# Spreading a hosted modulation chunk over both weight chunks of a feed-forward step, and over the last two chunks of a projection group

## The reference

```python
ada = jax.nn.silu(c) @ w_ada[l] + b_ada[l]              # first block, 6 x 1024 numbers per layer
sh1, sc1, g1, sh2, sc2, g2 = jnp.split(ada, 6, axis=-1)
...
h = x * (1.0 + sc2) + sh2
g, u = jnp.split(h @ w_in, 2, axis=-1)                  # feed-forward
y = (jax.nn.silu(g) * u) @ w_out
...
m = jax.nn.silu(cond) @ w_ada + b_ada                   # second block, 9 x 1024 numbers,
                                                        # for c and for c_ctx: two vectors
```

## Time and profile before

| | us |
|---|---|
| median of 3 runs | 2665.36 |
| lowest and highest | 2662.78, 2667.13 |
| profiled execution | 2660.99 |
| its span | 2659.1 |
| granted TensorE clock, mean | 0.988 of full speed |
| PE busy | 2518.5 (95%) |
| DVE busy | 1741.2 (65%) |
| ACT busy | 1085.0 (41%) |
| DMA packets, 16 engines | 413.85 MB, 156 GB/s over the span |

### The profile page before, as it was taken

How to read it: one execution, slowest core, us unless ns; L and a number is a source line. 1 busy time by engine, 2 the same in 40 slices (tenths; PEclk the granted TensorE clock), 3 DMA queues, 4 the chain that set the end, 5 groups by cost and what they waited for, 6 DMA issues and landing times.

```text
span 2659.1 us, 41471 instructions
## 1 busy us (share of the span) xinstructions
PE 2518.5 (95%) x16280; PEld 2145.2 (81%) x16280; DVE 1741.2 (65%) x3313; ACT 1085.0 (41%) x2119; POOL 136.7 (5%) x92
## 2 busy tenths in 40 slices
PE   4879999899999999999998999999999999999999
PEld 3858998888997888887766788888788887777998
DVE  7678777677777677546778756554665543678754
ACT  2445545445444333223356333332333323446554
POOL 1000100000100111000000011100011100000010
PEclk9989999999999999999999999999999999999999
DMA  8926876926662444444510444434344433613653
GB/s 285 282 100 211 273 246 196 281 75 203 211 223 89 153 168 162 140 137 131 152 33 10 143 150 143 143 122 132 111 143 143 139 110 132 156 64 117 217 180 122
DMA packets 354893, 413.85 MB, mean 156 GB/s; under 512 B 24754, under 2 KB 291931, under 8 KB 354635
## 3 DMA queue, kind: packets, MB, share of 16 engines
q1 hardware_dynamic: 352496, 404.13, 47.3%
q0 software_dynamic: 1120, 5.70, 0.6%
q10 hardware_dynamic: 1082, 1.38, 0.2%
HBM read 409.56 MB, written 5.27 MB: 156 GB/s over the span
## 4 chain that ended last, share of the span: by engine, by line
PE 80%; DVE 11%; DMA 4%; ACT 3%; issue 2%; SPq 0%; ACTq 0%; DVEq 0%
PE bank L901 79%; DVE ada_partial L1632 3%; DVE weight_lo L695 2%; PE bank L1208 2%; DMA raw_weights<-in_w_in_ab_dram 1%; DMA raw_weights<-in_w_in_cd_dram 1%; ACT weight_hi L1295 1%; DMA raw_weights<-in_w_ffn_in_dram 1%; DVE bank L1952 1%; DVE X L1856 0%; ACT H_hi L1396 0%; DVE rstd L1899 0%; DVE probs L1971 0%; ACT X L1403 0%; DVE bias L1903 0%
## 5 line engine op out<-in xcount | busy, mean ns | idle before, releaser
L695 DVE TENSOR_TENSOR weight_lo<-raw_weights,weight_hi 128x512 fp32r<-128x512 f32 x1024 | 771.2, 761 | 797.0 <-ACT weight_hi L1295 782.0
L1295 ACT ACTIVATE weight_hi<-raw_weights 128x512 fp32r<-128x512 f32 x1024 | 632.6, 629 | 1231.9 <-PE bank L901 1125.7
L901 PE MATMUL bank<-H_hi,weight_hi 128*128 128x256 f32 (+1 forms) x2832 | 954.9, 337 | 36.2 <-DVE weight_lo L695 19.2
L901 PE MATMUL bank<-H_lo,weight_hi 128*128 128x256 f32 (+1 forms) x2832 | 938.7, 331 | 0.0
L901 PE MATMUL bank<-H_hi,weight_lo 128*128 128x256 f32 (+1 forms) x2832 | 938.1, 331 | 0.0
L901 PEld LDWEIGHTS bank<-H_hi,weight_hi 128*128 128x128 f32 x2832 | 540.0, 191 | 122.1 <-issue 58.6
L901 PEld LDWEIGHTS bank<-H_hi,weight_lo 128*128 128x128 f32 x2832 | 540.2, 191 | 50.7
L901 PEld LDWEIGHTS bank<-H_lo,weight_hi 128*128 128x128 f32 x2832 | 540.6, 191 | 47.1 <-issue 0.5
L1632 DVE SCALAR_TENSOR_TENSOR ada_partial<-raw_weights,silu_c,ada_partial 128x512 f32<-128x512 f32 x616 | 442.0, 745 | 1.4 <-DVE ada_partial L1632 0.2
L901 PE MATMUL bank<-hidden_hi,weight_hi 128*128 128x256 f32 (+1 forms) x1056 | 356.5, 338 | 4.0 <-DVE weight_lo L695 4.0
L901 PE MATMUL bank<-hidden_hi,weight_lo 128*128 128x256 f32 (+1 forms) x1056 | 354.1, 335 | 0.0
(11 more groups left out here) (191 smaller groups left out, 1848.7 us busy)
## 6 DMA issues: line engine op xcount, KB each, us to landing
raw_weights<-in_w_ada_dram SPq DMA_DIRECT2D x120, 1024.0 KB, 5.6
raw_weights<-in_w_ffn_up_dram SPq DMA_DIRECT2D x88, 1024.0 KB, 5.6
raw_weights<-in_w_ffn_in_dram SPq DMA_DIRECT2D x44, 1024.0 KB, 6.1
raw_weights<-in_w_ffn_down_dram SPq DMA_DIRECT2D x32, 1024.0 KB, 5.0
raw_weights<-in_w_in_dram SPq DMA_DIRECT2D x18, 1024.0 KB, 5.9
raw_weights<-in_w_ffn_out_dram SPq DMA_DIRECT2D x16, 1024.0 KB, 7.7
raw_weights<-in_w_in_ab_dram SPq DMA_DIRECT2D x12, 1024.0 KB, 9.3
raw_weights<-in_w_in_cd_dram SPq DMA_DIRECT2D x12, 1024.0 KB, 8.3
```

Source lines behind the costliest of these rows:

```text
L695: eng.tensor_tensor(WL[:, p.g % SPLIT, 0:p.kt * CW].rearrange("p (t n) -> p t n", n=CW), raw_ap(ch.n, ch.kt, CW)[:, p.k0:p.k0 + p.kt, :], ...
L901: return pe.matmul(o, w, x, start=start, stop=stop, skip_group_check=True)
L1295: act.activation(WH[:, p.g % SPLIT, 0:p.kt * CW].rearrange("p (t n) -> p t n", n=CW), raw_ap(ch.n, ch.kt, CW)[:, p.k0:p.k0 + p.kt, :], ACT ...
```

## The change

In a hosted step of `ffn_in` without `more`, DVE reads the a chunk in eight shares over the g loop and the u loop, not in four over the g loop. With four row tiles and eight shares, every second share does one tile: those at the second and fourth piece of each loop. The slot is released after the last share, at the end of the u loop. The order of the chunks (g, a, u) is not changed. In `proj` the a chunk moves ahead of c1 in the chunk order (c0, a, c1, c2), on SP too, and DVE reads it in seven shares beside the splits of c1's and c2's loops; the last share stands behind the group's last split, as before. Steps with `more`, the stages with one chunk per group, and qkv are as before.

```diff
--- before.py
+++ after.py
@@ -535,9 +535,10 @@
             ready=act_ready.take(11), host=host)
         groups = []
         for m in range(4):
-            cs = [chunk("g", view(w_out), k, min(KC, NF - k), CW * m) for k in range(0, NF, KC)]
-            groups.append(Rows(chunks=cs, host=ada_chunk() if steps[-1].host and m < 3 else None,
-                               grp=group("dve")))
+            cs = [chunk("g", view(w_out), 0, KC, CW * m)]
+            a1 = ada_chunk() if steps[-1].host and m < 3 else None
+            cs += [chunk("g", view(w_out), k, min(KC, NF - k), CW * m) for k in range(KC, NF, KC)]
+            groups.append(Rows(chunks=cs, host=a1, grp=group("dve")))
         add("proj", hosted=len(ADA) if bare else None, n=n, groups=groups, ada=ada, gate=gate, half=half, hidden=True,
             first=first,
             ready=act_ready.total, x_out=x_ready.take(1), tile6=x_tile.take(1),
@@ -815,8 +816,8 @@
                 for g in s.groups:
                     for ch in g.chunks:
                         load_one(ch)
-                    if g.host:
-                        load_one(g.host)
+                        if g.host and ch is g.chunks[0]:
+                            load_one(g.host)
 
         sp.wait_ge(out_cp, 4)
         sp.dma_start(out.rearrange("a (q p) d -> p (a q) d", p=P), OUTR[:, :, :]).then_inc(out_dma, 16)
@@ -1636,13 +1637,13 @@
                 chain.wait(closed["acc"][nv - 1])
                 dve.sem_inc(ada_used, 1)
 
-        def ahead_of(at, f, host=None, hook=None):
+        def ahead_of(at, f, host=None, hook=None, first=0, parts=None):
 
             n = len(f(at.u).pieces)
             for i in range(n):
                 ahead(at, lambda k: f(k).pieces[i], split, late)
                 if host:
-                    ada(at, host, i, n)
+                    ada(at, host, first + i, parts or n)
                 if hook:
                     hook(i)
 
@@ -1809,8 +1810,15 @@
             n = s.n
 
             def step(at):
-                ahead_of(at, lambda k: s.steps[k].g, (lambda k: s.steps[k].host) if s.steps[at.u].host else None)
-                ahead_of(at, lambda k: s.steps[k].u, (lambda k: s.steps[k].more) if s.steps[at.u].more else None)
+                st = s.steps[at.u]
+                host = (lambda k: s.steps[k].host) if st.host else None
+                if st.more:
+                    ahead_of(at, lambda k: s.steps[k].g, host)
+                    ahead_of(at, lambda k: s.steps[k].u, lambda k: s.steps[k].more)
+                else:
+                    half = KC // PIECE
+                    ahead_of(at, lambda k: s.steps[k].g, host, None, 0, 2 * half)
+                    ahead_of(at, lambda k: s.steps[k].u, host, None, half, 2 * half)
                 used(at, lambda k: s.steps[k].u.pieces[-1])
                 dve.wait_ge(silu_g.sem, at(lambda k: s.silu + k + 1))
 
@@ -1831,8 +1839,13 @@
             dve.wait_ge(ada_out, s.need)
             for m, g in enumerate(s.groups):
                 last = g is s.groups[-1]
+                at, parts = 0, sum(len(ch.pieces) for ch in g.chunks[1:])
                 for ch in g.chunks:
-                    if last and ch is g.chunks[-1]:
+                    if s.hidden and not last:
+                        ahead_of(one, lambda _: ch, (lambda _: g.host) if g.host and ch is not g.chunks[0] else None, None,
+                                 at, parts)
+                        at += len(ch.pieces) if ch is not g.chunks[0] else 0
+                    elif last and ch is g.chunks[-1]:
                         n_ahead = len(ch.pieces) - 1
                         for i, p in enumerate(ch.pieces[:-1]):
                             ahead(one, lambda _: p, split, late)
```

## The result

The changed kernel takes 2785.7 us (median of 4, 2784.1 to 2791.1) against 2664.6 (median of 4); the ratio is 1.0457, interval 1.0445 to 1.0469. The forecast was 2753, slower, with a stated range of 2715 to 2790. The profiled execution took 2784.06, its span is 2782.2, 123.1 us more than before.

What follows compares the result with a forecast made beforehand. PE was taken as the bound, busy 95% of the span. Terms 39.9 + 18.1 + 20.9 + 8.8 - 9.9 + 10 = 88 us on 2661.0 gave 2749, median 2753; range 2715 to 2790, its own 2735 to 2775.

Steps and rivals of the forecast that it cites:

- rival B: 256-column gaps: the clock falls at every stall, 37 us instead of 10, 2780 us; chance 0.14.
- Release, landing, split: Hosted `ffn_in`, after PE finishes u (S): u' issued at S + 2.2 us, landing 5.3, splitting 1.4; PE starts at S + 8.9.
- (1): `ffn_in` at 256 columns: PE idles 2.85 us on average before u' at 14 places, 39.9 us.
- (2): `ffn_in` at 512 columns: u' ready at S + 9.6 us against 10.88, so 29 places cost 0.
- (3): `proj`: c1' queues behind a', PE waits; 18.1 us first layer, 20.9 second layer, 8.8 at 512 columns.
- (4): Second layer's steps and `proj`: spreading DVE's work may remove losses of 5.4 and 4.5 us, a 9.9 us gain.
- (5): 256 columns: PE's clock falls behind some of 22 gaps, 0.46 us each on average, 10 us.
- Rival A: Whole change: the slot is not what binds and spreading helps, 2655 us, faster; chance 0.03.
- Rival C: Hosted steps and `proj`: DMAs issued together share engines, so all land at about 8.4 us, 2851 us; chance 0.08.
- Rival E: Whole change: no difference, DMAs already late before and PE had unseen slack; chance 0.03.
- Rival D: `proj`: the queue is shorter than assumed, or c1' lands with a'; its cost is a third, 2721 us; chance 0.12.

## Why the prediction was right, and where not

The mechanism was right: SP waits for a's slot, the weights behind it land late, and PE waits at the forecast places. Its added waiting was 86 us; the forecast without the clock term, the gain taken off, was 78. The sum was 33 us short, mainly by the clock term, and only the allowance for rival B in the stated range covers the measured time.

- **Release, landing, split** (S + 2.2, 5.3, 1.4): right. The chain has 310.45 - 309.01 = 1.4 us from the start of DVE's split to the issue (0.67 earlier ACT's), 5.20 for the landing, and with the gaps filled every first-layer step is 14.7 to 15.3 against 14.66. The fit that the prediction quotes from the Trainium skill (DMA: Bandwidth & Descriptors, Anatomy of one DMA) is stated there for DMAs that GpSimd issues; SP issues these, and their 5.2 us decide.
- **(1)** 14 places at 256 columns: right in place and number. The places of the second layer and the last feed-forward show it best: steps 1 and 2 there are 16.8 to 18.3 us, and the later ones together are within 0.6 us of those before (+0.5 and -0.6). In size, PE idled 3.1 us in the mean of the first layer's ten, for 2.85 forecast. In the last feed-forward one gap was 4.1 us, because u' landed 6.5 us after its issue.
- **(2)** 512 columns covered: right. Steps are 21.76 and 22.60 as in the earlier trace rows in all three feed-forwards, but for two of the third (21.94 and 22.35), and no stage's ten steps take longer than before.
- **(3)** `proj`: right. 17.6 us in the first layer with the gaps filled, 18.1 forecast; 18.2 in the second, 16.4 forecast with the gain. At 512 columns 9.1 with the offsets of the first steps, 8.8 forecast.
- **(4)** The gain in the second layer: wrong for the steps, 5.4 us that did not come; for `proj` the 4.5 us came in the run with a last (5.1, of which some 0.5 are the later product ahead of it, as in the first layer). "Spread out, a loop of DVE is 5.7 us, and both losses may go" left out the column sums, the product and the first split, which takes 1.37 us beside an instruction of GpSimd (667.42 us in the run named next) and 0.69 without; with them DVE has 12.2 us of work in a hosted two-vector step (with a last and six shares, first run, it is busy almost without a pause from 667.4 to 679.6 us) against 11.5 of PE. And it overlooked what the last share is put ahead of. Second layer, after, DVE and ACT (start, us):

```profile
778.66 1.41 DVE L1633 SCALAR_TENSOR_TENSOR ada_partial<-raw_weights,silu_c,ada_partial 128x512 f32<-128x512 f32 x2
780.31 0.75 DVE L1828 TENSOR_TENSOR tmp<-tmp,bank 128x256 f32<-128x256 f32 x2 [0.24 <-PE bank L902]
782.36 3.17 DVE L696 TENSOR_TENSOR weight_lo<-raw_weights,weight_hi 128x512 fp32r<-128x512 f32 x4 [1.30 <-ACT weight_hi L1296]
```

```profile
781.18 0.63 ACT L1474 ACTIVATE hidden_hi<-tmp 128x512 fp32r<-128x512 f32 x1 [3.16 <-DVE tmp L1828]
781.72 2.18 ACT L1296 ACTIVATE weight_hi<-raw_weights 128x512 fp32r<-128x512 f32 x4
```

The product (780.31) waits behind the last share (778.66), ScalarE's `hidden_hi` (781.18) behind the product, and the next step's split (781.72) behind that, in one queue. Hosted steps end later by this and the next one earlier: pairs of 24.5 to 24.9 us, before 24.1 to 25.2. In the runs with six shares pairs shrank by some 0.5 us, and with less for DVE to do in the hosted step by 1.0.
- **(5)** The clock: the term that was mis-sized. 10 us were taken, 0.46 per gap, from the mean over 7 waits. Here the clock fell behind seven of ten gaps in the first layer, for 1.5 to 1.8 us each, and filling the gaps of all stages at 256 columns was worth 33.6 us. The slip is in the divisor: the 7 waits were ScalarE's, and PE idled less often and mostly for less. Waits of 446 to 510 us before the change:

```profile
PE bank L901 <- DVE weight_lo L695: 9.0, 5, 3.1
```

Three of the five are over 1 us (2.93, 1.80 and 3.10). The same 3.2 us over these three are 1.1 per gap, an estimate of 23 to 24 us for 22 gaps, where 10 were taken. Rival B (all 22, 37 us, 2780) was nearer, with 19 of 22, and the clock (some 24 us) and the missing gain (5) make most of the 33 us between 2753 and 2786. The Trainium skill (TensorE: Matmul & The Clock Gate, HAM oscillation — how this bites in real kernels) has the clock fall in every pass of an example loop, where a DMA wait follows each short run of matmuls; the trace agrees nearly, with 7 of 10.
- **Rival A** needed a landing within 2.2 us; the chain has 5.20 and 5.22. **Rival C** is out: with three DMAs issued within 1.1 us the first still lands after 5.2, and 512-column steps are unchanged. **Rival E** is out: no slack took up the waits. **Rival D** is out by (3).

Not settled: why three first-layer gaps of ten left the clock alone and seven didn't. In the changed kernel the three are the shortest (2.83, 2.84 and 2.85 us, the seven 3.15 to 3.28), which looks like an answer. But in the run of the feed-forward part alone the clock fell behind 2.78 (twice) and 2.83 us and not behind two of 3.13 us, so length alone doesn't decide it.

## What to carry to other kernels

When reads of a buffer are spread out to ease an engine, ask first what takes its slot next: in a ring served in order the last read, not the mean one, sets when that transfer starts, and every transfer queued behind it. If the spread is wanted, move the buffer in the ring so that its successor is needed late; that alone turned a loss of 4.6% into none, and with the last share out of the way of the product into a gain of 0.3%. A gap of some 3 us on TensorE should be priced with the fall of its clock behind it, here 1.5 to 1.8 us more in two gaps of three or oftener. Take that price per gap of TensorE, and not per wait of an engine that feeds it.

## What was not expected of the hardware

Matmuls that nobody reads made the kernel 33.6 us faster (2785.7 to 2752.1) though the weights came no earlier. And three DMAs of 1 MB issued 0.45 to 0.6 us apart land nearly one after the other. SP's issues of 310 to 312 us in the changed kernel:

```profile
L749 SPq DMA_DIRECT2D raw_weights<-in_w_ffn_in_dram x2: 367/450/533, 310.5 to 310.9; - x2
L749 SPq DMA_DIRECT2D raw_weights<-in_w_ada_dram x1: 1072/1072/1072, 311.5 to 311.5; - x1
...
DMA to landing us min/median/max: 5.2/7.7/9.9
```

u', g'' and a'' were issued at 310.5, 310.9 and 311.5 and landed 5.2, 7.7 and 9.9 us later, about 3 us apart; the first is as early as the first of a pair in the earlier trace rows. At 512 columns a batch issued from 1681.2 us landed after 5.3, 7.8 and 9.8 us, and the prediction allowed the first 6.6. That is what kept the 512-column steps whole.
